# The third attention branch's output products in fp32r, on pairs of chunks, in a two-block kernel on one core

## The reference

```
h = rms_norm(x, g_pre) * (1 + scale) + shift
cq, ckv, ..., zc, gcols = split(h @ w_in)
o_a = (mla_branch(...)  * silu(za)) @ w_o_mla
o_b = (swa_branch(...)  * silu(zb)) @ w_o_swa
o_c = (diff_branch(...) * silu(zc)) @ w_o_diff      # its rows are normed: rms_norm(o, g_sub) * (1 - lam_init)
g = sigmoid(gcols).reshape(B, S, 3, D)
y = (g[0] * o_a + g[1] * o_b + g[2] * o_c) @ w_out
x = x + gate * rms_norm(y, g_post)
```

## Time and profile before

| | us |
|---|---|
| three executions | 2118.18, 2122.26, 2121.98 |
| median | 2121.98 |
| the profiled execution: its time | 2116.54 |
| its span | 2114.6 |
| TensorE busy | 2073.5 (98%) |
| VectorE busy | 1616.8 (76%) |
| ScalarE busy | 1289.6 (61%) |
| third branch's products, first layer | 315.21 to 328.84 |
| third branch's products, second layer | 622.81 to 636.44 |

### The profile page before, as it was taken

How to read it: one execution, slowest core, us unless ns; L and a number is a source line. 1 busy time by engine, 2 the same in 40 slices (tenths; PEclk the granted TensorE clock), 3 DMA queues, 4 the chain that set the end, 5 groups by cost and what they waited for, 6 DMA issues and landing times.

```text
span 2114.6 us, 33307 instructions
## 1 busy us (share of the span) xinstructions
PE 2073.5 (98%) x12826; PEld 1864.1 (88%) x12826; DVE 1616.8 (76%) x1940; ACT 1289.6 (61%) x1568; POOL 74.8 (4%) x58
## 2 busy tenths in 40 slices
PE   6999999999999999999999999999999999999998
PEld 5899999999999989999999888888888888888886
DVE  6667986558885765555645988888898888888897
ACT  2645554655644754434634777777777777777776
POOL 0000000000000300000000000000000000000010
PEclk7999999999999999999999999999999999999999
DMA  9975455656335524553638999999999999999991
GB/s 291 249 239 175 159 148 138 146 184 196 113 126 174 162 81 160 180 180 122 204 106 338 379 374 387 371 383 380 367 389 355 390 375 386 380 376 374 367 393 73
DMA packets 315510, 548.07 MB, mean 259 GB/s; under 512 B 68364, under 2 KB 208577, under 8 KB 315401
## 3 DMA queue, kind: packets, MB, share of 16 engines
q1 hardware_dynamic: 306384, 530.81, 72.0%
q0 software_dynamic: 3168, 11.54, 1.8%
q10 hardware_dynamic: 5848, 4.19, 0.7%
HBM read 539.14 MB, written 7.36 MB: 258 GB/s over the span
## 4 chain that ended last, share of the span: by engine, by line
PE 94%; DVE 3%; ACT 1%; DMA 1%; issue 1%; ACTq 0%; SPq 0%; DVEq 0%
PE bank L729 27%; PE bank L731 26%; PE bank L730 26%; PE bank L676 2%; PE bank L882 2%; PE bank L1312 1%; PE bank L1421 1%; PE bank L689 1%; PE bank L714 1%; PE bank L865 1%; PE bank L851 1%; PE bank L855 1%; PE bank L853 1%; DVE piece_lo L2572 1%; DMA ring<-in_w_ada 1%
## 5 line engine op out<-in xcount | busy, mean ns | idle before, releaser
L2835 DVE TENSOR_TENSOR w_lo<-pool,w_hi 128x2048 fp32r<-128x2048 f32 x336 | 766.3, 2291 | 101.4 <-ACT w_hi L2055 100.2
L2055 ACT ACTIVATE w_hi<-pool 128x2048 fp32r<-128x2048 f32 x336 | 641.6, 1918 | 143.6 <-PE bank L731 143.6
L729 PE MATMUL bank<-w_hi,xe_hi 128*128 128x512 f32 x896 | 354.5, 396 | 0.0
L731 PE MATMUL bank<-w_hi,xe_lo 128*128 128x512 f32 x896 | 349.6, 390 | 0.0
L730 PE MATMUL bank<-w_lo,xe_hi 128*128 128x512 f32 x896 | 349.0, 390 | 0.0
L729 PE MATMUL bank<-h_upper,upper 128*128 128x256 f32 x1056 | 311.7, 295 | 3.2 <-DVE h_lo L2372 3.2
L730 PE MATMUL bank<-h_lo,upper 128*128 128x256 f32 x1056 | 299.2, 283 | 0.0
L731 PE MATMUL bank<-h_upper,ring_lo 128*128 128x256 f32 x1056 | 299.2, 283 | 0.0
L2273 DVE TENSOR_TENSOR ring_lo<-ring,upper 128x1024 fp32r<-128x1024 f32 x148 | 180.0, 1222 | 102.8 <-ACT upper L1573 102.3
L2572 DVE TENSOR_TENSOR piece_lo<-ring,piece_hi 128x1024 fp32r<-128x1024 f32 x118 | 145.0, 1237 | 96.5 <-ACT piece_hi L1562 96.2
L729 PEld LDWEIGHTS bank<-h_upper,upper 128*128 128x128 f32 x1056 | 202.7, 192 | 6.0 <-issue 4.1
(11 more groups left out here) (427 smaller groups left out, 3399.1 us busy)
## 6 DMA issues: line engine op xcount, KB each, us to landing
pool<-in_od_exp_w SPq DMA_DIRECT2D x336, 1024.0 KB, 7.5
ring<-in_w_in SPq DMA_DIRECT2D x48, 1024.0 KB, 5.4
ring<-in_ev_ffn_w SPq DMA_DIRECT2D x33, 1024.0 KB, 5.3
ring<-in_w_ada SPq DMA_DIRECT2D x24, 1024.0 KB, 6.4
ring<-in_od_w_in SPq DMA_DIRECT2D x12, 1024.0 KB, 6.2
ring<-in_ev_w_in SPq DMA_DIRECT2D x10, 1024.0 KB, 5.3
ring<-in_w_in SPq DMA_DIRECT2D x32, 256.0 KB, 4.6
ring<-in_w_out SPq DMA_DIRECT2D x8, 1024.0 KB, 5.0
```

Source lines behind the costliest of these rows:

```text
L729: nc.tensor.matmul(b, left[0], right[0], start=first, stop=False, skip_group_check=True)
L731: return nc.tensor.matmul(b, left[1], right[0], start=False, stop=last, skip_group_check=True)
L2055: nc.scalar.activation(w_hi[q % 3], ring_slot(q), ACT.Copy)\
L2835: V.tensor_tensor(w_lo[q % 3], ring_slot(q), w_hi[q % 3].bitcast(F32), ALU.subtract)\
```

## The change

Branch c goes the way of branches a and b: its weights join the list of split pieces, its rows are split (into the tiles of branch a's rows, which are free by then), and its products are three fp32r matmuls. In all three branches two chunks now share a bank of 512 columns, and VectorE gates, adds and splits them as one 128x512 operation; `tmp` and `probsT` take turns for the gated product. TensorE's token squares come before branch b, the spreads after chunks 1 and 2, the sub-norms on VectorE after pairs 0 and 1, the lower part of branch c's rows after pair 2. The splits of branch c's weight pieces take the places behind branch b's pairs; those of the first `w_out` pieces move into branch c, one behind each pair.

```
@@ uppers
-                [("wo" + br, l, i) for br in "ab" for i in range(2)] + [("out", l, i) for i in range(4)]:
+                [("wo" + br, l, i) for br in "abc" for i in range(2)] + [("out", l, i) for i in range(4)]:
@@ o_parts
-        return (oa_hi, oa_lo) if br == "a" else (h_upper, h_lo[:, 0:4])
+        return (h_upper, h_lo[:, 0:4]) if br == "b" else (oa_hi, oa_lo)
@@ TensorE: branch_out
+            tile, j = ("wo" + br, l, c // 4), c // 2 % 2
+            n, col = first[tile] + j, slice(P * (c % 2), P * (c % 2) + P)
+            if c == 0:
+                pe.wait_ge(o_split, when(o_split, br, l))
+            if c % 2 == 0:
+                pe.wait_ge(lower_ready, when(lower_ready, n))
+                wo_bank[br] = claim("gemm", ("wo" + br, l, c // 2), y_ready, br, l, c // 2)
+            hi, lo = upper_tile(n), upper_source(n)[1]
+            for k in range(4):
+                m = product(wo_bank[br][:, S * (c % 2):S * (c % 2) + S], (hi[:, k, col], lo[:, k, col]),
+                            [o_[:, k] for o_ in o_parts(br)], k == 0, k == 3)
+            if c % 2:
+                m.then_inc(psum_ready, wrote("wo" + br, l, c // 2))
+                upper_used[n] = ticks.counts["psum_ready"]
             if c % 4 == 3:
-                release("wo" + br, l, c // 4)
+                release(*tile)
@@ TensorE: the order of a layer
-            for c in range(2):
-                branch_out("b", l, c)
             b = claim("gemm", ("ms", "sub", l), rstd_ready, "sub", l)
             ...
-            for c in range(2, KD):
+            for c in range(KD):
                 branch_out("b", l, c)
-                if c in (3, 4):
-                    spread(("sub", l), 4 * (c - 3), 4, dve_step, "sub", l, 2 * (c - 3) + 1)
-            for c in range(4):
-                pe.wait_ge(o_ready, when(o_ready, "c", l, c))
+                if c in (1, 2):
+                    spread(("sub", l), 4 * (c - 1), 4, dve_step, "sub", l, 2 * (c - 1) + 1)
             for c in range(KD):
                 branch_out("c", l, c)
@@ ScalarE: upper_rows
-            act.wait_ge(o_ready, when(o_ready, "b", l, 7))
+            act.wait_ge(o_ready, when(o_ready, "c", l, 3) if br == "c" else when(o_ready, "b", l, 7))
+            if br == "c":
+                act.wait_ge(psum_ready, when(psum_ready, "woa", l, 3))
@@ ScalarE: the order of a layer
             token_root("sub", l, n=8)
-            for n in range(PIECES):
-                form_upper(first["out", l, 0] + n)
-            for c in range(KD):
-                act.wait_ge(y_ready, when(y_ready, "sum", l, c))
-                nc.scalar.activation(h_hi(c), gates[:, c], ACT.Copy).then_inc(h_upper_ready, tick(h_upper_ready, "y", l, c))
+            for n in range(2):
+                form_upper(first["woc", l, 0] + n)
+            upper_rows("c", l)
+            for n in range(2, PIECES):
+                form_upper(first["woc", l, 0] + n)
+            for c in range(0, KD, 2):
+                act.wait_ge(y_ready, when(y_ready, "sum", l, c // 2))
+                nc.scalar.activation(h_hi(c, 2), gates[:, c:c + 2], ACT.Copy)\
+                    .then_inc(h_upper_ready, two(h_upper_ready, "y", l, c))
+                form_upper(first["out", l, 0] + c // 2)
@@ VectorE: split_y
+        def split_y(l, n):
+            c, pair = 2 * n, slice(2 * n, 2 * n + 2)
+            dve.wait_ge(h_upper_ready, when(h_upper_ready, "y", l, c + 1))
+            V.tensor_tensor(h_lo[:, pair], gates[:, pair], h_hi(c, 2).bitcast(F32), ALU.subtract)\
+                .then_inc(h_split, two(h_split, "y", l, c))
@@ VectorE: branch_in
+            def branch_in(br, n):
+                b = psum(dve, "wo" + br, l, n)
+                pair = slice(2 * n, 2 * n + 2)
+                at_ = KD * "abc".index(br) + 2 * n
+                part = (tmp, probsT[:, 0])[n % 2]
+                V.scalar_tensor_tensor(gates[:, pair] if br == "a" else part, gates[:, at_:at_ + 2], 1.0,
+                                       b.rearrange("p (a s) -> p a s", a=2), ALU.add, ALU.mult)\
+                    .then_inc(y_ready, tick(y_ready, br, l, n))
+                if br != "a":
+                    dve.wait_ge(y_ready, when(y_ready, br, l, n))
+                    m = V.tensor_tensor(gates[:, pair], gates[:, pair], part, ALU.add)
                     if br == "c":
+                        m.then_inc(y_ready, tick(y_ready, "sum", l, n))
@@ VectorE: the order of a layer
+            for n in range(4):
+                branch_in("a", n)
+                if n == 0:
                     lower_rows("b", l)
+                if n > 0:
+                    lower((("wob", l, (n - 1) // 2), (n - 1) % 2))
             lower((("wob", l, 1), 1))
+            inverse_tokens("sub", l, n=8)
+            for n in range(4):
+                branch_in("b", n)
+                if n < 2:
+                    sub_norm(2 * n)
+                    sub_norm(2 * n + 1)
+                if n == 2:
+                    lower_rows("c", l)
+                if n > 0:
+                    lower((("woc", l, (n - 1) // 2), (n - 1) % 2))
+            lower((("woc", l, 1), 1))
+            for n in range(4):
+                branch_in("c", n)
+                if n > 0:
+                    split_y(l, n - 1)
+                    lower((("out", l, (n - 1) // 2), (n - 1) % 2))
+            split_y(l, 3)
+            lower((("out", l, 1), 1))
             lower(*both("out", l, 2), *both("out", l, 3))
```

More of the change, by code:

```diff
@@ L897, in run_units @@
                     values(us[n - 2])
-        wo_slot = {}
+        wo_bank = {}
         def branch_out(br, l, c):
[L902 to L923, removed]
+            tile, j = ("wo" + br, l, c // 4), c // 2 % 2
[12 more added lines that the diff above has]
+                upper_used[n] = ticks.counts["psum_ready"]
             if c % 4 == 3:
-                release("wo" + br, l, c // 4)
+                release(*tile)
         def modulation(l, i):
@@ L2505, in _ @@
                 gate_gain(1)
[L2507 to L2511, removed]
+            def branch_in(br, n):
[6 more added lines that the diff above has]
+                    .then_inc(y_ready, tick(y_ready, br, l, n))
                 if br != "a":
-                    dve.wait_ge(y_ready, when(y_ready, br, l, c))
-                    m = V.tensor_tensor(gates[:, c], gates[:, c], tmp[:, c % 2], ALU.add)
+                    dve.wait_ge(y_ready, when(y_ready, br, l, n))
+                    m = V.tensor_tensor(gates[:, pair], gates[:, pair], part, ALU.add)
                     if br == "c":
-                        m.then_inc(y_ready, tick(y_ready, "sum", l, c))
+                        m.then_inc(y_ready, tick(y_ready, "sum", l, n))
             def sub_norm(c):
@@ L2525, in sub_norm @@
                     .then_inc(o_ready, tick(o_ready, "c", l, c))
-            for c in range(KD):
-                branch_in("a", c)
-                if c == 0:
+            for n in range(4):
+                branch_in("a", n)
+                if n == 0:
                     lower_rows("b", l)
-                if c > 1 and c % 2 == 0:
-                    lower((("wob", l, (c // 2 - 1) // 2), (c // 2 - 1) % 2))
+                if n > 0:
+                    lower((("wob", l, (n - 1) // 2), (n - 1) % 2))
             lower((("wob", l, 1), 1))
[L2534 to L2549, removed]
+            inverse_tokens("sub", l, n=8)
[16 more added lines that the diff above has]
+            lower((("out", l, 1), 1))
             lower(*both("out", l, 2), *both("out", l, 3))
```

## The result

| | before | after |
|---|---|---|
| median of the executions, us | 2122.26 (5, 2118.18 to 2124.08) | 2132.56 (5, 2130.14 to 2136.82) |
| the profiled execution, us | 2116.54 | 2130.14 |
| its span | 2114.6 | 2128.0 |

The ratio is 1.0057, interval [1.0037, 1.0077]: slower by half a per cent, outside my range and 5.7 us above the forecast. Over all comparisons of this study, 74 executions, the kernel before has a median of 2121.5 (2116.5 to 2125.8), so the change costs about 11 us; with five executions of the kernel after, the interval allows 8 to 16.

What follows compares the result with a forecast made beforehand. TensorE, 98% busy, was taken as the bound, with VectorE setting its pace in the third branch. Per layer 2.37 us saved against waits of 1.3 and 3.2; 2.1 + 2.8 = 4.9 slower, median 2126.9, range 2119.5 to 2131.

Steps and rivals of the forecast that it cites:

- Spared products: Third branch on TensorE: 32 steps of three fp32r products take 11.52 us instead of 13.63, 2.11 less a layer.
- The 0.08 at the sums: Token squares beside the modulation sums, first layer: one start of 0.20 us saved in place of 0.12.
- VectorE's prices: VectorE's operation costs in the branches: 1.32 us a pair, between 1.20 and 1.39; 0.2 from its end to TensorE's restart.
- GpSimd's copy: Second layer: the copy falls on a VectorE with no idle time and costs 0 to 1.04 us, taken as 0.7.
- The waits: TensorE waits 1.3 us for the third branch's rows, 3.2 for the third output residue; net 2.1 and 2.8 a layer.
- rival (a): VectorE keeps no backlog and the copy misses; only work behind the last pair counts, 0.4 us a layer, 2122.8; chance 0.22.
- rival (c): The new TensorE waits cost clock, dropping it to 1.2 GHz: 2.8 us more over both layers, 2129.7; chance 0.10.
- the row at 717.78: Earlier trace: behind 2.00 us of TensorE idling the clock was 1.00, 2.4 GHz; taken as evidence against rival (c).

Runs made afterwards that it cites:

- e4: Changed kernel with the lower part of the third branch's rows split after pair 1 instead of pair 2; 2135.08 us, ratio 1.0065 to the kernel before.
- e7: Changed kernel with the edits of e2, e3 and e4 together; 2127.36 us, ratio 1.0027 to the kernel before.
- e10: e7 with five throw-away matmul pairs on TensorE ahead of its wait for the second output residue; 2123.88 us, ratio 1.0008 to the kernel before.
- e11: Changed kernel with two interleaved output chunks first instead of three, plus the sums, rows and wait edits of e3, e4 and e10; 2120.55 us, ratio 0.9996.
- e6: The changed kernel, unchanged, run once more for a second profile; 2134.43 us in one execution.
- e2: Changed kernel with VectorE's third output weight residue placed ahead of the third branch's last pair; 2127.47 us, ratio 1.0028 to the kernel before.
- e1: Changed kernel with 9 throw-away matmuls on TensorE ahead of its wait for the third output residue; 2125.97 us, ratio 1.0023 to the kernel before.
- e3: Changed kernel with the first layer's last modulation sums moved earlier, away from the token squares; 2134.57 us, ratio 1.0067 to the kernel before.
- e8: Kernel before with only VectorE's third output residue moved late, behind the last chunk's sum; 2126.09 us, ratio 1.0019 to the kernel before.
- e9: Kernel before with only VectorE's third output residue moved later, behind the last split of the sum too; 2129.76 us, ratio 1.0034.
- e5: The kernel before, unchanged, run once more for a second profile; 2126.14 us in one execution.

## Why the prediction was wrong in size and right in kind

- **Spared products**: right. 11.62 us with the restart, 0.12 apart; 2.01 less than before, where 2.11 was put. (The 0.08 at the sums exists in the first layer alone; the prediction counts it in both.)
- **VectorE's prices**: right for the pair. VectorE's timeline of the kernel after, first layer, then the second with GpSimd's copy:

```profile
329.32 0.68 DVE L2508 SCALAR_TENSOR_TENSOR tmp<-pool,bank 128x512 f32<-128x512 f32 x1
330.03 0.69 DVE L2513 TENSOR_TENSOR pool<-pool,tmp 128x512 f32<-128x512 f32 x1
...
333.70 0.68 DVE L2373 TENSOR_TENSOR h_lo<-pool,h_upper 128x512 fp32r<-128x512 f32 x1
334.31 1.22 DVE L2268 TENSOR_TENSOR ring_lo<-ring,upper 128x1024 fp32r<-128x1024 f32 x1
```

```profile
642.47 1.48 POOL L3038 COPY pool<-ring 128x1024 f32<-128x1024 f32 x1 [100.59 <-DMA ring<-in_ev_w_in]
643.68 0.81 DVE L2513 TENSOR_TENSOR pool<-pool,tmp 128x512 f32<-128x512 f32 x1
```

  The pair's two operations start 0.71 apart and the second passes on after 0.60 or so: 1.32 as put. The residue that TensorE waits for starts at 334.31, ends at 335.53, and TensorE starts at 335.58: 0.05 instead of the 0.2 put. But the first gap behind a wait is 0.22 instead of 0.12 (335.58 to 335.80), and the last record ahead of it lasts 0.16 beyond the usual distance, so a wait costs TensorE some 0.26 more than the idle time in brackets.
- **GpSimd's copy**: 0.7 put, 0.1 measured (0.81 instead of 0.69), and that is the luck of the moment. Where it fell on an operation of VectorE with two inputs from SBUF, that one grew, by most of what was left of the copy: a residue from 1.22 to 2.06 (e4, e7), a split of the sum from 0.68 to 1.53 and 1.52 (e10, e11), a sum from 0.69 to 0.81, 0.89 and 1.03 (after, e6, e2). The gate's product, with one input from a bank, kept its 0.68 beside it (after, e1, e3, e6). In the kernel after, the copy began beside a residue and lasted 1.48, and most of the rest fell on such a product. e7, second layer:

```profile
639.25 1.21 POOL L3037 COPY pool<-ring 128x1024 f32<-128x1024 f32 x1 [99.67 <-PE bank L731]
639.48 2.06 DVE L2264 TENSOR_TENSOR ring_lo<-ring,upper 128x1024 fp32r<-128x1024 f32 x1
```

- **The waits**: right. For the rows 1.3 was put; 1.05 of idling measured in both layers, 1.3 as a delay. For the third residue 3.2 was put and 3.9 in the second layer, against 2.43 and 2.44 of idling after short ones of 0.19 and 0.31 for the second; as delays, both residues together, 3.05 and 3.2. Net of what is spared: 2.0 and 2.2 us later than before at the third chunk, put 2.1 and 2.8. Together 4.2 for 4.9. This is the mechanism of the forecast, and rival (a) is out: VectorE did keep a backlog, as e4 shows.
- **The step that failed is the one that rejected rival (c)**, "by the row at 717.78 it doesn't". One row of one execution stood against it. In both profiles of the kernel after, the products behind the third chunk's wait ran at 1.2 GHz for 3.4 us, in both layers; 1.6 us a layer, near the 1.4 that the rival put. With it: 2126.9 + 3.2 = 2130.1, against 2132.56 measured. e1 and e10 take the clock's part away and leave the third chunk where it was; e8 and e9 make it come and go with nothing else changed. Over the thirteen profiles half clock followed all ten output projections with a wait of 2.30 to 2.44 and both of e7, and none of the other fourteen. The Trainium skill (TensorE: Matmul & The Clock Gate, section HAM oscillation) describes this, a wait between bursts of matmuls after which TensorE starts at half clock, for waits longer than these, so by the page alone the rival was no certainty; the trace agrees in kind (0.57 over 336 to 340 behind 2.43 us of idling). I gave the row more weight than it could carry: its place came out the other way in four of thirteen profiles.
- **Not foreseen: half clock at the first layer's second branch.** I noted that the squares would stand beside the modulation sums and counted only the 0.08 gained. The two groups of one-column matmuls together last 2.6 us, and behind them four of five profiles fell to 1.2 GHz, 1.6 us lost in three of them and about twice that in e2. Its share of the median is an estimate, 1.3 for four of five at 1.6, and e3 did not show it in the time.
- **Not foreseen: 0.8 us at 515.** ScalarE had a piece of the second layer's input weights 10.2 us later than before (504.81 to 514.99), where all else was 8.9 later, and TensorE waited 0.65 for it. Of the nine profiles with the change six have a delay of 0.8 to 0.9 there, e10 and e11 one of 0.3, and e1 none; the kernel before and its variants have none. I did not find out why.

The sum of these: 4.2 + 3.2 + 1.3 + 0.8 = 9.5 of the 11 us between the medians; the rest is open, as is part of what e1 gained.

## What to carry to other kernels

Where TensorE is the bound, shifting work from it to the next busiest engine gains only as long as that engine has slack in the same stage; count its sum over the stage before counting what TensorE is spared, and then ask what the first late result stands in front of. Price a new wait of TensorE twice: the idling and the clock behind it. If a wait of about two microseconds can't be moved away, throw-away matmuls in it cost nothing (e1, e10), and taking away the need (two chunks first instead of three) is better still. And one favourable row of one execution doesn't rule out a clock effect: profile the same kernel twice before you lean on it.

## What was not expected of the hardware

- The same program position with the same 2.00 us of idling kept the clock at 1.00 in nine profiles (the earlier trace rows among them) and was followed by 0.50 in four (e4, e7, e8, e10).
- Idling of 1.36 and 0.56 us close together, and of 1.71 and 0.57, was followed by half clock (e7); one of 1.74 alone was not, in either layer (e8); ones of 2.30 to 2.44 were, ten times of ten (after, e3, e4, e6, e9).
- Two groups of one-column matmuls side by side, with TensorE never idle by the records, were followed by half clock in four of five profiles.
- GpSimd's copy lengthened VectorE's operations with two SBUF inputs, by up to 0.85 us, and left the gate's product, which reads a bank, at 0.68.
- Two executions of an unchanged kernel differ by up to 9.6 us (e5 against the first profile), and half-clock stretches of 3.4 or 6.8 us between the layers make a part of that.
